# One core, 512 tokens, three layers in fp32 pairs: rotary angles earlier on VectorE, head norms of the second model part in another order, other counts of filler products at the layer norm

## The chip, the cores and the metric

The kernel runs on one core of one Trainium2 chip, as one program with one launch. The metric is the device time of that launch in microseconds, as the median of several runs. The five engines each work through an instruction stream of their own: TensorE (PE; its weight loads are listed as PEld), VectorE (DVE), ScalarE (ACT), GpSimd (POOL) and SyncE (SP), which here issues all transfers. They wait for each other through semaphores.

## The reference, cut to what matters

All of it is float32. x has 512 tokens of 1024 features.

```python
h = rms_norm(x, g[0])
proj = h @ w_in                      # gates, xs, q_lat (384), kv_lat (256), k_rope (32)
y_a  = gate_b * depthwise_conv(gate_c * xs, sc_kernel)
q    = rms_norm(q_lat, q_norm) @ w_uq
kv   = rms_norm(kv_lat, kv_norm) @ w_ukv
ang  = positions[..., None] * inv_freq
cos, sin = jnp.cos(ang), jnp.sin(ang)   # rotate q_pe and k_rope
x = x + rms_norm(concat(y_a, attention) @ w_out, g[1]);  x = x + rms_norm(mlp(...), g[3])
...
# second layer
u = a * sigmoid(g);  u = depthwise_conv(u, w_dw, 31 taps) + b_dw
u = silu(layer_norm(u, ln_g, ln_b));  m = u @ w_pw2 + b_pw2      # then rms_norm, mlp as above
...
# a third layer, behind 16 meta tokens
q, k, v, fg, u = split(rms_norm(h) @ w_in_2)
q, k = rms_norm over each head of 64;  cum_logf = cumsum(log_sigmoid(fg + b_fgate))
p_out = pool_scale * ((trailing_mean(u, 2/4/8/16) - u) @ w_pool)
h = h + concat(forgetting_attention(q, k, v, cum_logf), p_out) @ w_out;  h = h + swiglu(...)
```

## The kernel before

Everything is kept transposed: 128 features on the partitions, 512 tokens along the free axis. A weight block is 128 x 1024 floats (8 tiles of 128 x 128). For the precision each operand is held as a rounded high part and a low part, and a product of two tiles is three matmuls of 128 x 512 (`products`, L1646 to L1648): high x high, high x low, low x high. A weight block goes through a ring of four: SP loads `raw`, ScalarE rounds it to `wh` (`hi`), GpSimd subtracts to get `wl` (`lo`), TensorE uses both. A weight tile times all of x is 24 matmuls (`tile`). The results stand in four PSUM banks in turn; a tile can start when the one four tiles before it has been read out (`open_tile`, semaphore `bank_free`).

A norm is made of a few short steps that several engines share: the squares are summed to `ssq` (ScalarE and VectorE or GpSimd), TensorE sums over the partitions (`stat`, L1676), ScalarE takes the root (`root`, `latent_root`), VectorE the reciprocal (`factor`, L1081), and TensorE spreads the factors over the partitions (`spread`, L1688) with four matmuls (eight records, since these are fp32). `stat` and `spread` stand as hooks at hand-written places inside tiles. Where TensorE would have nothing to do, `keep_busy` issues products of an identity matrix into a spare bank (L1656); the counts are the constants `W_...` in one line (L126).

The order on each engine is written by hand; nothing is scheduled. Three places matter here.

The first is the start. VectorE makes the rotary angles (`angle`, L1054 to L1060 by its helpers): six or seven operations on 128 x 512, once for the cosine (`angle(0, 0.25)`, seven operations) and once for the sine (`angle(1, 0.0)`, six). Between the two it computes the reciprocal for x (`factor("x0")`) as soon as ScalarE has the root. Behind both stand the sums of squares of the latent q (`sum_squares`, L1052), which `stat("q_lat")` in tile 4 of w_in waits for. `spread("x0")`, earlier in tile 4, waits for that reciprocal. ScalarE's `latent_out` squares wait for x's sum.

The second is the layer norm in front of `pw2`. TensorE sums the mean (L1959), keeps busy (`W_CENTRE`), sums the squares over the features in four steps of four (L1976; GpSimd adds the pairs, L588), keeps busy for three (`W_FACTOR`), spreads, keeps busy for sixteen (`W_UPDATE`), and enters pw2. VectorE and ScalarE make the operand parts XH and XL of eight tiles meanwhile; `enter` runs three output tiles together over the input tiles as these arrive.

The third is w_in_2 of the third model part. Its tiles 0 to 3 are q of two heads each, tile 4 the forget gate (`log_forget`, `prefix_sums`), tiles 5 to 8 the pooled branch (`pool_tile`), 9 and 10 and two more in w_in_2b k of two heads each. Each of the eight head tiles needs a norm of its own: `head_square` and `head_root` (ScalarE), `head_stat` (TensorE, L2006), `head_factor` (VectorE, writes `hexp`, L1481 and L1482), `head_spread` (TensorE, L2017), `head_norm` (VectorE, L1060), `head_round` (ScalarE, L950), `head_low` (VectorE, L1060). TensorE's parts are hooks: head_stat(1) at k=2 and head_spread(1) at k=6 of tile 5, head_stat(2) and head_spread(2) at k=2 and k=7 of tile 6, head_stat(3) at k=4 of tile 7, head_spread(3) at k=2 of tile 8. head_stat(e) also waits for head_norm(e-1). Between tile 10 and w_in_2b stands the pool product: four groups of three matmuls into four banks, one `blocks_done` behind all; `pool_out` on VectorE scales the four results into `tmp` and `sqb` and frees the banks. The first tile of w_in_2b needs the first of these banks.

```python
            angle(0, 0.25)
            factor("x0")
            step(stt(floor[:], sd[:], EPS, sd[:], ALU.mult, ALU.mult))
            angle(1, 0.0)
```

Of the kernel before, what the change touches and what calls it, by code (L numbers as in the profile page):

```python
# [27 lines left out]
ALU = mybir.AluOpType  # L28
# [55 lines left out]
BLOCK0, TILE0 = {}, {}  # L84
# [38 lines left out]
HEAD_TILE = [TILE0["w_in_2"] + i for i in (0, 1, 2, 3, 9, 10)] + [TILE0["w_in_2b"] + i for i in range(2)]  # L123


W_STAT, W_FACTOR, W_UPDATE, W_MEAN, W_CENTRE, W_VALUES, W_START, W_GATE, W_WARM = 10, 3, 16, 10, 10, (1, 1), 20, 10, 8  # L126
P_OUT_STEPS = 4
Y_FREE = TILE0["w_in"] + 15

# [1 line left out]
def build(nc, x_t, meta_t, positions, vectors, weights, out_t):  # L131
    ctx = ExitStack()
    with ctx:
# [3 lines left out]
        def sem(name):  # L137
            return ctx.enter_context(nc.semaphore(name))
# [187 lines left out]
        p_out_h, p_out_l = sem("p_out_h"), sem("p_out_l")  # L326
        fz, fexp, cum_done, decay_q = sem("fz"), sem("fexp"), sem("cum_done"), sem("decay_q")
        pooled_done, pool_hi, pool_lo = sem("pooled_done"), sem("pool_hi"), sem("pool_lo")
        decay_ones, meta_zero = sem("decay_ones"), sem("meta_zero")
        decay_k = [sem(f"decay_k{e}") for e in range(HEADS // 2)]  # L330
        out_done = sem("out_done")
# [284 lines left out]
        def _(sc):  # L616
# [7 lines left out]
            def hi(n):  # L624
                if n >= NBLK:
                    return
                j = n % RING
                sc.wait_ge(raw_in[j], 16 * (n // RING + 1))
                if n >= RING:
                    sc.wait_ge(blocks_done, n - RING + 1)  # L630
                sc.activation(wh[:, j], raw[:, j], ACT.Copy).then_inc(w_hi, 1)  # L631
# [288 lines left out]
            def head_square(e):  # L920
                keys = e >= 4
                w = L2 if keys else S
                sc.wait_ge(bank_free, HEAD_TILE[e] + 1)
                if e:
                    sc.wait_ge(hstat, e)
                sc.activation(head_q[:, 0:w], head_t[:, e % 4, 0:w], ACT.Square).then_inc(hsq, 1)

            def head_root(e):

                keys = e >= 4  # L930
                scale = 1.0 if keys else float(HD)
                sc.wait_ge(hstat, e + 1)
                sc.activation(hcol[:, 0, 0:8], PS[:, STAT, 0:8], ACT.Sqrt, bias=EPS * scale,
                              scale=scale / HD).then_inc(act if keys else hsd, 1)
                if keys:
                    chain[0] += 1
                    sc.activation(hcol[0:META, 0, 8:10], PS[0:META, STAT, 8:10], ACT.Sqrt, bias=EPS * scale,
                                  scale=scale / HD).then_inc(hsd, 1)
# [15 lines left out]
            head_square(1)  # L954
            head_round(0)
            hi(n0 + 8)
            sc.wait_ge(fz, 1)
            sc.activation(logf[:, 1], logf[:, 1], ACT.Exp, scale=-1.0).then_inc(act, 1)
            chain[0] += 1
            sc.wait_ge(act, chain[0])  # L960
            sc.activation(logf[:, 1], logf[:, 1], ACT.Ln, bias=1.0).then_inc(fexp, 1)
            head_root(1)
            head_square(2)
            head_round(1)
            hi(n0 + 9)
            head_root(2)
# [70 lines left out]
        def _(v):  # L1037
# [8 lines left out]
            def sig(ins, s, n):  # L1046

                ins.then_inc(s, 1)
                v.wait_ge(s, n)
# [70 lines left out]
            def angle(i, shift):  # L1120

                step(ts(turns[:], ang[:], 0.15915494309189535, ALU.mult, shift, ALU.add))
                step(ts(turns[:], turns[:], 12582912.0, ALU.add, -12582912.0, ALU.add))
                for part in (6.28125, 0.0019350051879882812, 3.019916050461616e-07):
                    step(stt(trig[:, i], turns[:], -part, (ang if part > 6 else trig[:, i])[:], ALU.mult, ALU.add))
                if shift:
                    step(ts(trig[:, i], trig[:, i], 1.5707963267948966, ALU.add))
                sig(ts(trig[:, i], trig[:, i], 3.1415925, ALU.min, -3.1415925, ALU.max), angles, i + 1)
# [15 lines left out]
            step(v.tensor_copy(ang[:], pos_i[:]))  # L1144
            step(ts(ang[:], ang[:], col("inv_freq"), ALU.mult))
            angle(0, 0.25)
            factor("x0")
            step(stt(floor[:], sd[:], EPS, sd[:], ALU.mult, ALU.mult))
            angle(1, 0.0)

            T0, n0 = TILE0["w_in"], BLOCK0["w_in"]

# [395 lines left out]
                sig(stt(pooled[:, i], pool_a[:, i % 2, META:L2], 1.0 / w, u2[:, META:L2], ALU.mult, ALU.subtract),  # L1548
                    pooled_done, i + 1)

            def pool_out():

                for i in range(4):
                    T = TILE0["pool"] + i
                    v.wait_ge(blocks_done, BLOCK0["pool"] + 1)
                    sig(ts(p_out(i), PS[:, T % 4], col("pool_scale", i), ALU.mult), bank_free, T + 1)

            for e in range(4):
                head_in(e, "w_in_2", e)
# [5 lines left out]
            head_norm(1)  # L1565
            pool_tile(0)
            head_low(1)
            prefix_sums()
            head_factor(2)
            head_norm(2)  # L1570
            pool_tile(1)
            head_low(2)
# [6 lines left out]
            head_factor(4)  # L1579
            head_norm(4)  # L1580
            head_in(5, "w_in_2", 10)
            head_low(4)
            pool_out()
            head_factor(5)
            head_norm(5)
            head_in(6, "w_in_2b", 0)
# [56 lines left out]
        def _(pe):  # L1643
# [332 lines left out]
                    ins = pe.matmul(PS[:, STAT, j:j + 1], ln_sq[:, 2 * i, j * P:(j + 1) * P], ones[:, 0:1],  # L1976
                                    start=i == j == 0, stop=(i, j) == (LN_PAIRS - 1, 3))
            ins.then_inc(stat_done, 1)
            keep_busy(W_FACTOR, spare)
            spread("ln")  # L1980
            keep_busy(W_UPDATE, spare)
            enter("pw2", "ln")
            for m in range(4, KT):
                tile(BLOCK0["pw2"] + m, TILE0["pw2"] + m)
# [46 lines left out]
            for i in range(4):  # L2031
# [1 line left out]
                pe.wait_ge(pool_hi, i + 1)  # L2033
                pe.wait_ge(pool_lo, i + 1)
                ins = products(PS[:, (T1 + i) % 4], *weight(n1, i), pool_h[:, i], pool_l[:, i], True, True)
            ins.then_inc(blocks_done, 1)
            n0, T0 = BLOCK0["w_in_2b"], TILE0["w_in_2b"]
            for i in range(2):
                tile(n0 + i, T0 + i, {3: head(5 + i)[0], 6: head(5 + i)[1]}, meta_out=T0 + i)
# [203 lines left out]
```

## Time and profile before

| what | value |
|---|---|
| median of 3 runs | 1880.98 us (1879.87 to 1881.52) |
| the profiled execution | 1879.82 us |
| its span, first to last instruction | 1878.0 us |
| busy in the span: PE / DVE / ACT / POOL | 1820.3 / 809.6 / 636.8 / 900.8 us |
| granted TensorE clock, mean | 0.985 of full speed |

The page counts how long each engine worked, and follows the chain of waits back from the last instruction. A matmul of 128 x 512 is shown with 0.39 us, but such matmuls overlap, and in the chain each takes 0.23 us at full clock; at half clock 0.43 us. TensorE's granted clock stands per stretch: 1.00 is 2.4 GHz, 0.50 is 1.2 GHz. A wait in brackets at the end of a row, [1.64 <-DVE hexp L1482], says how long the engine was idle before and what ended that.

### The profile page before, as it was taken

Reading aid. Unit: us, or ns where it says so; the run is one execution under the profiler, and the core shown is the slowest. Engines: PE = TensorE matmul, PEld = TensorE weight load, DVE = VectorE, ACT = ScalarE, POOL = GpSimd, SP = SyncE. Lnnn points to the kernel's source line nnn. Section 1 sums busy time; section 2 is a strip of 40 time slices with the busy share of each in tenths; the row PEclk is TensorE's granted clock in tenths of the full one; section 3 lists DMA queues with packets and bytes.
Section 4 is the critical chain, followed back from the end, with each engine's and each line's share of the span. In section 5 each row is a group of like instructions: output and inputs, shape, how many; then the busy total and the mean of one; then the engine's idle time right before and its main releaser. Section 6 shows DMA issues by size and latency. Waiting matters only on the chain.

```text
span 1878.0 us, 23679 instructions
## 1 busy us (share of the span) xinstructions
PE 1820.3 (97%) x8511; PEld 1506.6 (80%) x8511; DVE 809.6 (43%) x1238; ACT 636.8 (34%) x954; POOL 900.8 (48%) x478
## 2 busy tenths in 40 slices
PE   7999999999999989999999999998998999999999
PEld 5787887888888768787888888887878778888887
DVE  7447645301321478855520232256546154444200
ACT  5327525222321444444321222252245242222221
POOL 5346445444444479954444444453243354444443
PEclk9999999999999989999999999998999999999999
DMA  5332022233232213221322322310210223322332
GB/s 176 85 121 68 12 90 79 90 101 96 93 101 92 66 56 102 68 88 61 109 95 95 101 91 99 100 57 24 81 57 1 68 68 101 101 94 96 101 103 76
DMA packets 45925, 157.87 MB, mean 84 GB/s; under 512 B 5728, under 2 KB 5984, under 8 KB 45856
## 3 DMA queue, kind: packets, MB, share of 16 engines
q1 hardware_dynamic: 45856, 156.93, 26.4%
q8 instruction: 46, 0.75, 0.2%
q14 instruction: 23, 0.19, 0.0%
HBM read 152.58 MB, written 2.10 MB: 82 GB/s over the span
## 4 chain that ended last, share of the span: by engine, by line
PE 86%; POOL 5%; DVE 5%; issue 2%; ACT 2%; DMA 0%; SPq 0%; POOLq 0%; DVEq 0%; ACTq 0%
PE PS L1646 27%; PE PS L1647 26%; PE PS L1648 26%; POOL acc_p L539 2%; PE PS L1656 2%; POOL wl L528 2%; PE PS L1857 1%; PE PS L1688 1%; PE PS L1676 1%; DVE PS L1060 1%; POOL acc_p L567 1%; PE PS L2017 1%; POOL UL L556 0%; DVE tmp L1060 0%; DVE XL L1052 0%
## 5 line engine op out<-in xcount | busy, mean ns | idle before, releaser
L475 POOL TENSOR_TENSOR wl<-raw,wh 128x1024 fp32r<-128x1024 f32 x232 | 563.0, 2428 | 677.0 <-ACT wh L645 293.1
L1646 PE MATMUL PS<-XH,wh 128*128 128x512 f32 x1408 | 561.2, 399 | 14.8 <-DVE PS L1056 5.0
L1647 PE MATMUL PS<-XL,wh 128*128 128x512 f32 x1408 | 552.3, 392 | 0.0
L1648 PE MATMUL PS<-XH,wl 128*128 128x512 f32 x1408 | 551.9, 392 | 0.0
L1646 PEld LDWEIGHTS PS<-XH,wh 128*128 128x128 f32 x1408 | 267.0, 190 | 78.5 <-issue 12.4
L1648 PEld LDWEIGHTS PS<-XH,wl 128*128 128x128 f32 x1408 | 266.7, 189 | 56.9
L1647 PEld LDWEIGHTS PS<-XL,wh 128*128 128x128 f32 x1408 | 267.0, 190 | 52.6
L1646 PE MATMUL PS<-HH,wh 128*128 128x512 f32 x688 | 267.6, 389 | 0.0
L1647 PE MATMUL PS<-HL,wh 128*128 128x512 f32 x688 | 267.6, 389 | 0.0
L1648 PE MATMUL PS<-HH,wl 128*128 128x512 f32 x688 | 267.6, 389 | 0.0
L645 ACT ACTIVATE wh<-raw 128x1024 fp32r<-128x1024 f32 x96 | 101.6, 1061 | 405.0 <-PE PS L1648 405.0
L1052 DVE TENSOR_TENSOR tmp<-PS,r 128x512 f32<-128x512 f32 x116 | 79.9, 691 | 236.2 <-PE PS L1648 215.9
L631 ACT ACTIVATE wh<-raw 128x1024 fp32r<-128x1024 f32 x94 | 98.6, 1055 | 154.6 <-PE PS L1648 146.0
L1648 PEld LDWEIGHTS PS<-HH,wl 128*128 128x128 f32 x688 | 129.1, 188 | 26.8
L1646 PEld LDWEIGHTS PS<-HH,wh 128*128 128x128 f32 x688 | 129.1, 188 | 26.8
L1647 PEld LDWEIGHTS PS<-HL,wh 128*128 128x128 f32 x688 | 129.1, 188 | 26.8
L466 POOL TENSOR_TENSOR wl<-raw,wh 128x1024 fp32r<-128x1024 f32 x33 | 80.5, 2446 | 131.1 <-ACT wh L631 131.0
L864 ACT ACTIVATE wh<-raw 128x1024 fp32r<-128x1024 f32 x56 | 59.4, 1060 | 164.2 <-PE PS L1648 164.2
L1031 ACT ACTIVATE wh<-raw 128x1024 fp32r<-128x1024 f32 x40 | 42.5, 1062 | 159.0 <-PE PS L1648 159.0
L496 POOL TENSOR_TENSOR prob<-prob,cols 128x512 f32<-128x512 f32 (+2 forms) x64 | 57.5, 901 | 64.4 <-DVE cols L1266 64.1
L1356 DVE COPY M<-PS 128x512 f32 x16 | 11.1, 692 | 158.6 <-PE PS L1648 158.6
L1052 DVE TENSOR_TENSOR X<-X,PS 128x512 f32<-128x512 f32 x16 | 11.0, 687 | 148.5 <-PE PS L1648 148.5
(310 smaller groups left out, 2302.0 us busy)
## 6 DMA issues: line engine op xcount, KB each, us to landing
raw<-weights SPq DMA_DIRECT2D x286, 512.0 KB, 3.5
X<-x_t SPq DMA_DIRECT2D x8, 256.0 KB, 6.8
out_t<-X SPq DMA_DIRECT2D x8, 256.0 KB, 4.4
KH<-rope_h SPq DMA_DIRECT2D x4, 128.0 KB, 4.6
KL<-rope_l SPq DMA_DIRECT2D x4, 128.0 KB, 5.3
QH<-XH SPq DMA_DIRECT2D x16, 32.0 KB, 2.0
QL<-XL SPq DMA_DIRECT2D x16, 32.0 KB, 2.0
pos_i<-positions SPq DMA_DIRECT2D x1, 256.0 KB, 9.3
```

Of the source, the lines that this page charges most:

```text
L466: pool.tensor_tensor(wl[:, n % RING], raw[:, n % RING], wh[:, n % RING].bitcast(F32), ALU.subtract).then_inc(w_lo, 1)
L475: pool.tensor_tensor(wl[:, j], raw[:, j], wh[:, j].bitcast(F32), ALU.subtract).then_inc(w_lo, 1)
L496: pool.tensor_tensor(p, p, cols[:, u % 4, 2:3].broadcast_to(p.shape), ALU.mult).then_inc(p_done, 1)
L528: pool.tensor_tensor(wl[:, i % RING], raw[:, i % RING], wh[:, i % RING].bitcast(F32), ALU.subtract).then_inc(w_lo, 1)
L631: sc.activation(wh[:, j], raw[:, j], ACT.Copy).then_inc(w_hi, 1)
L645: sc.activation(wh[:, j], raw[:, j], ACT.Copy).then_inc(w_hi, 1)
L864: sc.activation(wh[:, slot], raw[:, slot], ACT.Copy).then_inc(w_hi, 1)
L1031: sc.activation(wh[:, slot], raw[:, slot], ACT.Copy).then_inc(w_hi, 1)
L1052: return v.tensor_tensor(out, a, b, op)
L1646: pe.matmul(out, wa, xa, start=start, stop=False)
L1647: pe.matmul(out, wa, xb, start=False, stop=False)
L1648: return pe.matmul(out, wb, xa, start=False, stop=stop)
```

## The change

Five edits:

1. VectorE: `angle(1, 0.0)` is placed in front of `factor("x0")` and the `floor` operation, straight behind `angle(0, 0.25)`.
2. TensorE at the layer norm: `W_CENTRE` 16 for 10; the three products behind the squares' sum are dropped; the count behind the spread is `W_GATE` (10) for `W_UPDATE` (16).
3. ScalarE at w_in_2: head_root(1) and head_square(2) stand in front of the forget gate's Exp and Ln.
4. VectorE at w_in_2: head_factor(2) stands in front of `prefix_sums`, which now lies between head_factor(2) and head_norm(2).
5. The pool product counts each of its first three groups on a semaphore of its own (`pool_mixed`), and VectorE reads the results one by one, two of them in front of head_low(4), two behind it.

```diff
-W_STAT, W_FACTOR, W_UPDATE, W_MEAN, W_CENTRE, W_VALUES, W_START, W_GATE, W_WARM = 10, 3, 16, 10, 10, (1, 1), 20, 10, 8
+W_STAT, W_FACTOR, W_UPDATE, W_MEAN, W_CENTRE, W_VALUES, W_START, W_GATE, W_WARM = 10, 3, 16, 10, 16, (1, 1), 20, 10, 8
...
             head_round(0)
             hi(n0 + 8)
+            head_root(1)
+            head_square(2)
             sc.wait_ge(fz, 1)
             sc.activation(logf[:, 1], logf[:, 1], ACT.Exp, scale=-1.0).then_inc(act, 1)
...
             sc.activation(logf[:, 1], logf[:, 1], ACT.Ln, bias=1.0).then_inc(fexp, 1)
-            head_root(1)
-            head_square(2)
             head_round(1)
...
             angle(0, 0.25)
+            angle(1, 0.0)
             factor("x0")
             step(stt(floor[:], sd[:], EPS, sd[:], ALU.mult, ALU.mult))
-            angle(1, 0.0)
...
-            def pool_out():
-
-                for i in range(4):
-                    T = TILE0["pool"] + i
+            def pool_out(i):
+
+                T = TILE0["pool"] + i
+                if i == 3:
                     v.wait_ge(blocks_done, BLOCK0["pool"] + 1)
-                    sig(ts(p_out(i), PS[:, T % 4], col("pool_scale", i), ALU.mult), bank_free, T + 1)
+                else:
+                    v.wait_ge(pool_mixed, i + 1)
+                sig(ts(p_out(i), PS[:, T % 4], col("pool_scale", i), ALU.mult), bank_free, T + 1)
...
             head_low(1)
+            head_factor(2)
             prefix_sums()
-            head_factor(2)
             head_norm(2)
...
             head_in(5, "w_in_2", 10)
+            pool_out(0)
+            pool_out(1)
             head_low(4)
-            pool_out()
+            pool_out(2)
+            pool_out(3)
             head_factor(5)
...
             ins.then_inc(stat_done, 1)
-            keep_busy(W_FACTOR, spare)
             spread("ln")
-            keep_busy(W_UPDATE, spare)
+            keep_busy(W_GATE, spare)
             enter("pw2", "ln")
...
                 ins = products(PS[:, (T1 + i) % 4], *weight(n1, i), pool_h[:, i], pool_l[:, i], True, True)
-            ins.then_inc(blocks_done, 1)
+                ins.then_inc(blocks_done if i == 3 else pool_mixed, 1)
```

Where instructions move, the instruction streams show it. VectorE at the start, from the end of the first angle set to the sums of squares of the latent q; first before, then the change (its line numbers are one higher). `rcol` is x's factor, `turns` and `tmp` are the angles, `ssq` the sum.

```order
L1057 TENSOR_SCALAR tmp<-tmp 128x512
L1081 RECIPROCAL rcol<-sd 128x4
L1060 SCALAR_TENSOR_TENSOR floor<-sd 128x4
L1057 TENSOR_SCALAR turns<-ang 128x512
L1057 TENSOR_SCALAR turns<-turns 128x512
L1060 SCALAR_TENSOR_TENSOR tmp<-turns,ang 128x512
L1060 SCALAR_TENSOR_TENSOR tmp<-turns,tmp 128x512 x2
L1057 TENSOR_SCALAR tmp<-tmp 128x512
L1052 TENSOR_TENSOR PS<-PS,sqb 128x512
L1052 TENSOR_TENSOR ssq<-PS,sqb 128x512
```

```order
L1058 TENSOR_SCALAR tmp<-tmp 128x512
L1058 TENSOR_SCALAR turns<-ang 128x512
L1058 TENSOR_SCALAR turns<-turns 128x512
L1061 SCALAR_TENSOR_TENSOR tmp<-turns,ang 128x512
L1061 SCALAR_TENSOR_TENSOR tmp<-turns,tmp 128x512 x2
L1058 TENSOR_SCALAR tmp<-tmp 128x512
L1082 RECIPROCAL rcol<-sd 128x4
L1061 SCALAR_TENSOR_TENSOR floor<-sd 128x4
L1053 TENSOR_TENSOR PS<-PS,sqb 128x512
L1053 TENSOR_TENSOR ssq<-PS,sqb 128x512
```

The reciprocal and `floor` moved behind the six operations of the second set; nothing was added or taken away.

ScalarE at w_in_2, behind the first head's rounding; before, then the change. `hcol` is a head's root, `head_q` the squares of the next head, `logf` the forget gate's Exp and Ln, and ACT_TABLE_LOAD the load of another set of function tables.

```order
L631 ACTIVATE wh<-raw 128x1024
L958 ACT_TABLE_LOAD
L958 ACTIVATE logf<-logf 8x528
L961 ACT_TABLE_LOAD
L961 ACTIVATE logf<-logf 8x528
L933 ACT_TABLE_LOAD
L933 ACTIVATE hcol<-PS 128x8
L926 ACTIVATE head_q<-head_t 128x512
L950 ACTIVATE Q2H<-PS,headones 128x512 x2
L631 ACTIVATE wh<-raw 128x1024
L933 ACTIVATE hcol<-PS 128x8
```

```order
L632 ACTIVATE wh<-raw 128x1024
L934 ACTIVATE hcol<-PS 128x8
L927 ACTIVATE head_q<-head_t 128x512
L961 ACT_TABLE_LOAD
L961 ACTIVATE logf<-logf 8x528
L964 ACT_TABLE_LOAD
L964 ACTIVATE logf<-logf 8x528
L951 ACTIVATE Q2H<-PS,headones 128x512 x2
L632 ACTIVATE wh<-raw 128x1024
L934 ACT_TABLE_LOAD
L934 ACTIVATE hcol<-PS 128x8
```

The root of head tile 1 is now ahead of the three table loads; there are still three, the last of them in front of the root of head tile 2.

VectorE at w_in_2, between head_low(1) and head_norm(2); before, then the change. `hcol` and `hexp` are head_factor(2), the `logf` and `decay` rows are `prefix_sums`, the last row is head_norm(2).

```order
L1060 SCALAR_TENSOR_TENSOR logf<-logf 8x528
L1529 MEMSET logf 8x528
L1530 SCALAR_TENSOR_TENSOR logf<-logf 8x528
L1532 CAST decay<-logf 8x528
L1052 TENSOR_TENSOR decay<-logf,decay 8x528
L1481 RECIPROCAL hcol<-hcol 128x8
L1482 COPY hexp<-hcol 128x512
L1060 SCALAR_TENSOR_TENSOR PS<-head_t,vec,PS 128x512
```

```order
L1482 RECIPROCAL hcol<-hcol 128x8
L1483 COPY hexp<-hcol 128x512
L1061 SCALAR_TENSOR_TENSOR logf<-logf 8x528
L1530 MEMSET logf 8x528
L1531 SCALAR_TENSOR_TENSOR logf<-logf 8x528
L1533 CAST decay<-logf 8x528
L1053 TENSOR_TENSOR decay<-logf,decay 8x528
L1061 SCALAR_TENSOR_TENSOR PS<-head_t,vec,PS 128x512
```

The two operations of head_factor(2) went ahead of the five of the prefix sums.

## Rows read from the trace of the kernel before

**Rows 1.** Waits of PE, whole span: us in total, times, longest us.
```profile
PE PS L1676 <- DVE ssq L1052: 7.4, 1, 7.4
...
PE PS L2017 <- DVE hexp L1482: 4.8, 2, 3.2
...
PE PS L1646 <- DVE tmp L1056: 1.7, 1, 1.7
```

**Rows 2.** Timeline of DVE, 18 to 50 us: start us, us, line, operation, idle before.
```profile
27.57 0.69 DVE L1060 SCALAR_TENSOR_TENSOR tmp<-turns,ang 128x512 f32<-128x512 f32 x1
...
36.00 0.18 DVE L1081 RECIPROCAL rcol<-sd 128x4 f32<-128x4 f32 x1 [5.36 <-ACT sd L657]
...
42.14 5.46 DVE L1060 SCALAR_TENSOR_TENSOR tmp<-turns,tmp 128x512 f32<-128x512 f32 x2
...
48.83 0.69 DVE L1052 TENSOR_TENSOR ssq<-PS,sqb 128x512 f32<-128x512 f32 x1
```

**Rows 3.** Windows of PE at the start: us, busy (x), granted clock, DMA.
```profile
44.90:55.20 10.30, 5.62 (x17) 0.50 0.33 102
```

**Rows 4.** Timeline of POOL, 10 to 50 us.
```profile
32.74 2.40 POOL L466 TENSOR_TENSOR wl<-raw,wh 128x1024 fp32r<-128x1024 f32 x1 [13.99 <-ACT wh L631]
...
37.06 1.97 POOL L483 MEMSET KL<- 32x2048 f32 x1
```

**Rows 5.** Timeline of PE, 38 to 40 us: x's spread.
```profile
39.10 1.05 PE L1688 MATMUL PS<-ident,rcol 128*128 128x128 f32 x8
```

**Rows 6.** The chain in order of time, whole span: start us, us, what.
```profile
276.65 3.64 PE PS L1656 x16
...
807.06 1.49 PE PS L1656 x3
808.55 1.71 PE PS L1688 x8
810.26 4.96 PE PS L1656 x16
```

**Rows 7.** Timeline of DVE at the layer norm, 790 to 822 us.
```profile
807.30 0.18 DVE L1081 RECIPROCAL rcol<-sd 128x4 f32<-128x4 f32 x1 [3.86 <-ACT sd L657]
...
812.43 0.69 DVE L1052 TENSOR_TENSOR XL<-PS,XH 128x512 fp32r<-128x512 f32 x1 [0.73 <-ACT XH L912]
```

**Rows 8.** Windows of PE at the layer norm.
```profile
806.00:812.90 6.90, 6.90 (x24) 0.51 0.41 131
```

**Rows 9.** The chain, 1254 to 1296 us, third model part.
```profile
1264.43 1.28 ACT L958
...
1268.35 1.28 ACT L933
...
1270.64 2.08 PE PS L2017 x8
...
1281.94 0.99 DVE logf L1060
...
1286.80 1.58 PE PS L2017 x8
...
1295.27 0.79 PE PS L2006 x8
```

**Rows 10.** Windows of PE in the third model part.
```profile
1270.30:1273.70 3.40, 3.06 (x11) 0.50 0.00 0
...
1287.30:1294.20 6.90, 6.90 (x24) 0.51 0.00 0
```

**Rows 11.** Timeline of PE, 1254 to 1274 us: head_stat(1).
```profile
1263.96 0.95 PE L2006 MATMUL PS<-headones,head_q 128*128 128x2 f32 x8
```

**Rows 12.** Timeline of DVE, 1256 to 1345 us.
```profile
1329.80 0.69 DVE L1052 TENSOR_TENSOR head_t<-PS,r 128x512 f32<-128x512 f32 x1
...
1333.18 1.54 DVE L1056 TENSOR_SCALAR tmp<-PS,vec 128x512 f32<-128x512 f32 x2
```

**Rows 13.** Windows of PE behind the pool product.
```profile
1334.10:1340.00 5.90, 5.90 (x34) 1.00 0.62 180
```

More of the change, by code:

```diff
@@ L328, in build @@
         pooled_done, pool_hi, pool_lo = sem("pooled_done"), sem("pool_hi"), sem("pool_lo")
+        pool_mixed = sem("pool_mixed")
         decay_ones, meta_zero = sem("decay_ones"), sem("meta_zero")
```

## The prediction, made before the kernel ran

> **What bounds the kernel now.** I first read the page's shares: TensorE is busy for 1820.3 of the span's 1878.0 us, and the chain of waits runs through it almost everywhere. So a change can win in two ways only: a wait of TensorE that goes, or time in which its clock stands at half. I then listed the waits of TensorE by what ended them, and looked for those that the edits touch [rows 1]: 7.4 us for the latent q's sum of squares, 4.8 us in two waits for head factors (3.2 and 1.6), 1.7 us for the first scaled pool result. Last I read the granted clock around each. The reader is to see that a wait costs more than its length: behind it TensorE works at half clock for a while, and the same work at full clock takes half the time. VectorE is busy for 43% only; it matters by its order. A difference of 0.2% (3.8 us) is about what a measurement of this kernel can tell from none.
>
> **Part A, the angles.** VectorE has nothing to do for 5.36 us before x's factor, from 30.64 to 36.00 us, then makes the second angle set until 48.07, and the latent sums end at 49.52 [rows 2]. TensorE waits for them 7.4 us [rows 1], from 42.2 to 49.58. The clock is at 0.50 from 44.9 to 55.2 us [rows 3]; of that TensorE works 5.6 us, which would take 2.8 at full clock. So at most 7.4 + 2.8 = 10.2 us are to be had. To have all of it, the second set must be through before x's spread, which TensorE reaches at 38.9 [rows 5], with the sums before 42.2. The six operations cost 11.8 us where they stand now, but only since GpSimd works beside them: a scalar_tensor_tensor takes 0.69 us with GpSimd idle and 2.7 with GpSimd at work [rows 2]. GpSimd is idle until 32.74, then has a subtraction (2.40) and two memsets, the second 1.97 [rows 4]. From 30.66 the first four operations (two of about 0.45, two of 0.7) end near 33.0; the fifth waits for the subtraction and ends near 35.8; the sixth waits for the first memset and ends near 37.8. Factor and floor follow by 38.1, 0.8 us ahead of TensorE; the sums (1.45) have all they need from ScalarE by 39.8 and end near 41.3, 0.9 us ahead. **A = 10.2 us.** The bounds are 3.9 us, if the six take 11.8 us here too (they end at 42.5, the spread resumes at 42.7 and the latent statistic comes at 45.7), and 10.5, if the stretch at half clock has more in it than the windows show. I take the upper side since GpSimd's two idle microseconds at 30.7 are in the rows.
>
> The page GPSIMD Engine Reference of the Trainium skill, section Key points, says that GpSimd's SBUF interfaces are shared with VectorE, for VectorE instructions in a two-port mode or with two SBUF inputs. By it the angle operations collide, as the 2.7 us show, while the sums, which read PSUM, do not. If a memset, which reads nothing, did not collide either, the sixth operation would end 1.5 us earlier, and the sum would be the same.
>
> **Part B, the layer norm.** Six more products of `W_CENTRE` stand in time that waits for GpSimd's additions anyway: nothing. The squares' statistic ends at 807.06; then come three fillers (1.49), the spread (1.71), sixteen fillers (4.96, until 815.22) [rows 6]. The factor is there at 807.48 [rows 7], so without the three fillers the spread starts at 807.5 instead of 808.55: 1.05 us. It ends at 809.2. The clock is at 0.51 until 812.9 [rows 8]. Ten fillers at half clock (0.43 each, twice the 0.23 of 3.64 / 16 [rows 6]) end at 813.5; with the clock back at 812.9 as now, at 813.2. XL's first tile is ready at 813.12 now [rows 7], 1.05 earlier then, so pw2 can start. **B = 815.2 - 813.2 = 2.0 us.** The bounds are 1.7 (all at half clock) and 3.1 (TensorE waits for XL alone, at 812.1).
>
> **Part C, w_in_2.** *First spread.* ScalarE's chain of three table loads and the forget gate's two functions runs from 1264.43 to 1269.63, and the root that TensorE needs stands behind it [rows 9]. head_stat(1) is done at 1264.9 [rows 11]. With the root ahead, ScalarE gives it at 1265.1, VectorE finishes head_low(0) at 1266.4, and head_factor(1), its copy held up by GpSimd's subtraction, ends by 1267.5; TensorE comes at 1269.0 (1270.64 less 1.64). The wait of 1.6 us goes, and with it 3.06 us of work at half clock [rows 10], worth 1.5: 3.1 us. *Second spread.* VectorE's prefix sums and head_factor(2) fill 1281.94 to 1286.80 [rows 9], 4.9 us, of which the factor is 0.7. In a frame shifted by the 3.1 us, TensorE comes at 1280.5 and VectorE ends head_low(1) at 1278.8; the factor is there at 1279.6, 0.9 us early. The wait of 3.2 us goes and 6.90 us at half clock [rows 10], worth 3.4: 6.6 us. *What is late next:* head_norm(2) now stands behind the prefix sums, 1279.6 + 4.2 + 0.8 = 1284.6, and head_stat(3) waits for it. TensorE gets there 8.5 us behind the spread now (1286.80 to 1295.27 [rows 9]), 5.0 at full clock: 1285.5, again 0.9 us of slack. The third table load moves in front of head_root(2), which comes 0.2 us late by it, hidden by VectorE's later work. The forget gate's results come at 1269.6, ten us before VectorE asks. Prefix sums that end later delay only the decay rows, which are sent behind the fourth head tile and are needed by the attention. *Pool results.* The first tile of w_in_2b waits 1.7 us for the first scaled result [rows 1], which VectorE starts at 1333.18, behind head_low(4). Now it may start when head_in(5) ends at 1330.5 [rows 12], takes 0.77 and is out at 1331.3, before TensorE's 1332.4. head_low(4) is put off by 1.5 us, to 1334.7, and head_spread(5), which needs it, comes after 1339. The clock behind this wait is 1.00 [rows 13], so no more is won: 1.7 us. **C = 3.1 + 6.6 + 1.7 = 11.4 us.** The bounds are 1.7 (a new wait in the place of each) and 12.
>
> **Sum.** 10.2 + 2.0 + 11.4 = 23.6 us off the profiled execution's 1879.82 gives 1856.2; the median of the runs stands 1.2 us above that execution, so 1857.4 us.
>
> **The rivals.** *R1, VectorE becomes the bound in w_in_2.* Both slacks there are 0.9 us, and one more collision with GpSimd costs 2. For it: VectorE's row of pool and head operations is dense, and the prefix sums stand in front of everything that follows. Against it: ScalarE, GpSimd and TensorE all move up together. TensorE would then wait about 1.1 us, and the clock falls again, worth 3.4 as now: 4.5 us given back, 1861.9.
>
> *R2, GpSimd holds up the second angle set.* A falls to its lower bound of 3.9, with 6.3 given back: 1863.7. For it: the six took 11.8 us. Against it: only three GpSimd operations stand before 39 us, and VectorE starts two us ahead of the first.
>
> *R3, the edits do what they say but the clock falls at other places.* That is the slower case. A wait of 1.64 us at 1269 halved the clock [rows 10], an equal one at 1332 did not [rows 13]: which one does is a matter of where it falls. Moving 1850 us of program against the clock's switching could put falls in stretches that have none now (short waits in the attentions, at the layer boundaries). Each costs up to 3.4 us, as the stretch at 1287; from the seventh on the gain of 23.6 is gone, and eight give 1857.4 + 27.2 = 1884.6. For it: nothing that I can see in the rows. Against it: as many falls can go as come. The page TensorE: Matmul & The Clock Gate of the Trainium skill, section Part 1, says that the gate watches on a free-running beat that a kernel's start does not reset; by that rule the number of falls differs from run to run, and the 1.7 us between the three runs before leave little room for it.
>
> *R4, the clock does better.* By the same switching the fall at the layer norm, or one elsewhere, is shorter: B at its upper bound and one fall of 1.5 to 3.4 us less, 1853 to 1855.
>
> **How the numbers follow.** My forecast (1855 to 1860.5) has 0.67. R1 has 0.14, R2 0.08, R4 0.08, R3 0.02; 0.01 is left for no difference at all. The likeliest gives 1857. The range goes from 1853, R4's lower end, to 1864. Each case has an us or two of spread of its own, by the bounds of B and by where the clock switches, so of R4 and of R2, whose centres lie at the two ends, about half is inside; with the forecast and R1 that makes 0.85 or so. Faster by over 0.2% are all but R3 and the rest: 0.97. Within 0.2%: 0.01. Slower: 0.02.
>
> **What would show it.** Right: no wait of TensorE for `ssq` in the first 60 us and clock 1.00 there; `rcol` by 38.2 us; the layer norm's ten fillers end some 2 us earlier behind the statistic; no wait for `hexp`, clock 1.00 or nearly so through w_in_2; no wait for `tmp` at the first tile of w_in_2b. Wrong: TensorE waiting at x's spread (R2); a new wait at head_stat(3) or head_spread(3) for `head_n` or `hexp`, with a half-clock stretch behind it (R1); a lower mean clock than 0.985 with all these waits gone (R3). With no wait removed the mean clock would stay where it is; I expect 0.99 or more. The forecast is wrong as a whole if the waits go but the next engine's work, a weight's low part or a transfer, ends the same distance later; the rows show GpSimd and DMA with room at all three places.

## The result: 1863.6 us, and where the time went

The changed kernel took 1863.62 us (median of six runs, 1860.05 to 1870.37), the kernel before beside it 1881.25 us: a ratio of 0.9911, 95% interval 0.9894 to 0.9928. That is 17 us less, on the side that was forecast; the forecast was 1857, some 7 us too low. The time lies at the upper end of the range (1864): the ratio, laid on the 1880.98 us from which the forecast was made, gives 1864.2, just outside. The six runs are of two groups, four from 1860.05 to 1864.43 and two at 1870. The profiled execution took 1864.43 us, 8.2 more than the 1856.2 that the sum gave for it. Its span is 1862.6 us and its mean granted clock 0.990 (0.985 before).

The waits of TensorE over the whole span, for what [rows 1] showed (us in total, times, longest):

```profile
PE PS L1652 <- DVE sqb L1057: 2.6, 1, 2.6
...
PE PS L1652 <- DVE head_t L1053: 1.0, 1, 1.0
```

The waits for `ssq` at the start (7.4 us) and for `hexp` (4.8 in two) are gone, and so is the one for `tmp` (1.7). In its place stands a longer one, 2.6 us for `sqb`, the third pool result. The 1.0 us for `head_t` was there before too.

Next the chain of work that ended last (start us, us, what), at the points where it can be laid beside the chain before. Of the changed kernel:

```profile
33.73 1.59 PE PS L1752 x7
...
267.51 3.64 PE PS L1662 x16
...
796.43 1.23 PE PS L1982 x8
798.12 2.07 PE PS L1694 x8
800.20 4.11 PE PS L1662 x10
...
1243.89 0.79 PE PS L2011 x8
...
1274.56 0.79 PE PS L2011 x8
...
1300.40 0.98 PE PS L2011 x8
...
1330.58 0.98 PE PS L2011 x8
```

And of the kernel before, what the rows above leave out:

```profile
32.64 1.59 PE PS L1746 x7
...
805.60 1.46 PE PS L1976 x8
...
1254.79 0.79 PE PS L2006 x8
...
1321.10 0.98 PE PS L2006 x8
...
1347.27 0.98 PE PS L2006 x8
```

Subtract line from line. In this run the first work on x starts 1.09 us later than before, ahead of everything that was changed. The sixteen fillers of [rows 6] moved from 276.65 to 267.51: 9.14 us, so part A is 10.2 net of that. From the squares' statistic to pw2 it was 9.62 us (805.60 to 815.22) and is 7.88 (796.43 to 804.31): part B is 1.74. Over w_in_2's head tiles the distance to before grows from 10.90 (1254.79 less 1243.89) to 20.71 us (1295.27 [rows 9] less 1274.56): 9.8 for the two `hexp` waits. It is still 20.70 at head_stat(4), 1321.10 less 1300.40. At head_stat(6) it is 16.69 (1347.27 less 1330.58), and at the end of the span 15.4. So everything came until 1300 us, and 4.0 + 1.3 us were given back behind it.

TensorE where they were given back (start, us, line, operation, idle before), in the first tile of w_in_2b:

```profile
1315.97 0.39 PE L1654 MATMUL PS<-XH,wl 128*128 128x512 f32 x1
1318.93 0.28 PE L1652 MATMUL PS<-meta_h,wh 128*128 128x16 f32 x1 [2.57 <-DVE sqb L1057]
...
1320.41 0.63 PE L1653 MATMUL PS<-XL,wh 128*128 128x512 f32 x1
```

VectorE in front of that wait, and GpSimd beside it:

```profile
1309.82 1.54 DVE L1057 TENSOR_SCALAR tmp<-PS,vec 128x512 f32<-128x512 f32 x2
1311.39 0.23 DVE L1057 TENSOR_SCALAR K2H<-head_t,headones 128x16 fp32r<-128x16 f32 x1
1311.67 2.26 DVE L1061 SCALAR_TENSOR_TENSOR K2L<-head_t,headones,K2H 128x16 fp32r<-128x16 f32 x1
1313.96 2.29 DVE L1057 TENSOR_SCALAR K2H<-head_t,headones 128x16 fp32r<-128x16 f32 x1
1316.28 0.23 DVE L1061 SCALAR_TENSOR_TENSOR K2L<-head_t,headones,K2H 128x16 fp32r<-128x16 f32 x1
1316.56 1.54 DVE L1061 SCALAR_TENSOR_TENSOR K2L<-PS,headones,K2H 128x512 fp32r<-128x512 f32 x2
1318.13 1.54 DVE L1057 TENSOR_SCALAR sqb<-PS,vec 128x512 f32<-128x512 f32 x2
```

```profile
1311.49 4.73 POOL L467 TENSOR_TENSOR wl<-raw,wh 128x1024 fp32r<-128x1024 f32 x2 [8.30 <-ACT wh L632]
```

Two things are to be seen. First, the matmul that waits is narrow, 16 columns of `meta_h`: the tile computes the meta tokens' columns too, from its fifth step on. In front of the first of them stands a wait, unchanged by the edits:

```python
                        if k == KT // 2:
                            pe.wait_ge(bank_free, meta_out - 1)
```

`bank_free` counts the read-outs in the order of the tiles, and this asks for all of them up to the tile two before. For w_in_2b's first tile that is the pool product's third result, and its read-out now stands behind head_low(4). The matmuls don't need that bank: the meta columns go to banks 5 and 7 in turn (`meta_bank`), the pool results stand in banks 0 to 3. It is the count that makes TensorE wait; a kernel that asks for a smaller count was not run.

Second, head_low(4) itself got longer. Its first four operations are only 128 x 16; two of them take 2.3 us, beside GpSimd's two subtractions, which start at 1311.49. Before, the same four stood ahead of GpSimd's start (1332.20), and VectorE's timeline had them at 0.23 and 0.24 us each:

```profile
1330.53 0.23 DVE L1056 TENSOR_SCALAR K2H<-head_t,headones 128x16 fp32r<-128x16 f32 x1
1330.80 0.24 DVE L1060 SCALAR_TENSOR_TENSOR K2L<-head_t,headones,K2H 128x16 fp32r<-128x16 f32 x1
...
1334.75 1.54 DVE L1056 TENSOR_SCALAR sqb<-PS,vec 128x512 f32<-128x512 f32 x2
```

```profile
1332.20 4.71 POOL L466 TENSOR_TENSOR wl<-raw,wh 128x1024 fp32r<-128x1024 f32 x2 [8.30 <-ACT wh L631]
```

The row at 1334.75 is the third and fourth pool result, the one below it GpSimd's two subtractions.

The page GPSIMD Engine Reference of the Trainium skill, section Key points, names the forms that collide with GpSimd: two SBUF inputs, or a two-port mode. The trace agrees for K2L, which has two SBUF inputs (`head_t` and `K2H`), and for operations that read PSUM: in the kernel before, `tmp` and `sqb` (1333.18 and 1334.75) take 0.77 us each beside the two subtractions, and in the version with the small operations first, below, the two large `K2L` take 1.54 together (from 1314.12). The blocked K2H has one SBUF input, `head_t`; that it ran in a two-port mode, no row says.

The clock behind the wait (windows of TensorE: us, busy (x), granted clock, DMA):

```profile
1319.70:1326.10 6.40, 6.40 (x24) 0.50 0.45 168
1340.00:1342.70 2.70, 2.68 (x6) 0.50 0.00 0
```

6.4 us at half clock cost 3.2. With the wait 0.9 us longer than the one it replaces, that is the 4.0 us. A second fall, 2.7 us long, stands behind the 1.0 us wait for `head_t` and costs the last 1.3. It does not come from the fifth edit: the kernel without it, below, has it too.

### The profile page after: what moved, and what is told of

The parts are those of the page before. It is cut to its first block, busy times and chain, and to the rows that moved or that the text cites. A ratio compares the mean times of both kernels' runs of the same rounds, so it can differ in the third digit from the quotient of the medians.

```text
span 1862.6 us, 23673 instructions
## 1 busy us (share of the span) xinstructions
PE 1817.0 (98%) x8508; PEld 1503.9 (81%) x8508; DVE 806.4 (43%) x1238; ACT 636.6 (34%) x954; POOL 899.8 (48%) x478
## 4 chain that ended last, share of the span: by engine, by line
PE 87%; POOL 5%; DVE 4%; issue 2%; ACT 1%; DMA 0%; SPq 0%; POOLq 0%; DVEq 0%; ACTq 0%
PE PS L1652 27%; PE PS L1654 27%; PE PS L1653 27%; POOL acc_p L540 2%; PE PS L1662 2%; POOL wl L529 2%; PE PS L1863 1%; PE PS L1694 1%; POOL acc_p L568 1%; DVE PS L1061 1%; PE PS L1682 1%; POOL UL L557 1%; PE PS L2022 0%; PE PS L1745 0%; DVE XL L1053 0%
```

## The experiments

Each part alone first. The four kernels ran on one chip and have the same runs of the kernel before beside them (median 1880.51 us).

**The angles alone** (edit 1).

```diff
             angle(0, 0.25)
+            angle(1, 0.0)
             factor("x0")
             step(stt(floor[:], sd[:], EPS, sd[:], ALU.mult, ALU.mult))
-            angle(1, 0.0)
```

> The kernel before with the first edit alone (second angle set ahead of x's factor). Theory 1 (the sum of part A: 7.4 us of waiting and 2.8 us of half clock): 10.2 us less, about 1871; no wait of TensorE for ssq in the first 60 us, clock 1.00 there, x's spread on time. Rival (GpSimd holds up the six operations): 4 us less, about 1877, with a wait at x's spread.

1870.75 us (1869.58 to 1877.61), ratio 0.9952, interval 0.9938 to 0.9966: 9.0 us. Three of its nine runs were at 1875 to 1878. The profiled one was among these, and its window from the first `hexp` wait (which this kernel still has) shows why:

```profile
1261.90:1291.80 29.90, 29.90 (x100) 0.50 0.05 18
```

Behind a wait of 1.64 us TensorE stayed at half clock for 29.9 us, where [rows 10] had 3.4. In most runs it did not.

**The layer norm alone** (edit 2).

```diff
-... W_CENTRE = 10
+... W_CENTRE = 16
-            keep_busy(W_FACTOR, spare)
             spread("ln")
-            keep_busy(W_UPDATE, spare)
+            keep_busy(W_GATE, spare)
```

> The kernel before with the second edit alone (filler counts at the layer norm). Theory 1: the spread starts 1.05 us earlier and ten fillers at about half clock end 1.7 to 2.0 us earlier behind the squares' statistic; 1879.2 us. Rival (the clock is worse without the fillers): half clock reaches into pw2's products, and the time is that of before or 1 us above. From the one first profile of the change the gain is 1.7.

1876.89 us, ratio 0.9980, interval 0.9961 to 0.9998: 3.8 us with 0.4 to 7 possible. The chain gives the size that the times can't. From 806.73 to pw2 at 814.61 it is 7.88 us, as in the whole change:

```profile
806.73 1.20 PE PS L1976 x8
808.39 2.08 PE PS L1688 x8
810.47 4.14 PE PS L1656 x10
```

**The head norms alone** (edits 3 and 4).

```diff
             hi(n0 + 8)
+            head_root(1)
+            head_square(2)
             sc.wait_ge(fz, 1)
...
-            head_root(1)
-            head_square(2)
             head_round(1)
...
+            head_factor(2)
             prefix_sums()
-            head_factor(2)
```

> The kernel before with edits 3 and 4 alone (root of head tile 1 ahead of the forget gate, factor of head tile 2 ahead of the prefix sums). Theory 1: both waits for hexp (4.8 us) go and with them 10 us at half clock, 9.7 us less, about 1871. Rival: one new wait at head_stat(3) or head_spread(3) with a fall of the clock, 5 us less.

1869.73 us (1868.48 to 1870.58), ratio 0.9936, interval 0.9914 to 0.9959: 12.0 us, against 9.8 by the trace of the whole change, which is inside the interval. No wait for `hexp` is left.

**The pool results alone** (edit 5).

```diff
             head_in(5, "w_in_2", 10)
+            pool_out(0)
+            pool_out(1)
             head_low(4)
-            pool_out()
+            pool_out(2)
+            pool_out(3)
```

> The kernel before with the fifth edit alone (pool results read one by one, two ahead of head_low(4)). Theory 1 (the meta columns of w_in_2b's first tile wait for the third pool result, which stands behind head_low(4), and that is held up by GpSimd's two subtractions): the wait of 1.7 us at the tile's start goes, one of about 2.5 us comes in its middle, and the clock falls behind it: 0.9 + 3.2 = about 4 us slower, 1885. Rival (the wait seen in the changed kernel was an effect of everything else having moved): 1.7 us less, 1879.3, no wait in the tile's middle.

1883.80 us (1881.84 to 1891.25), ratio 1.0018, interval 1.0006 to 1.0031: this part alone makes the kernel slower, by 3.4 us, where 1.7 were to be won. Its waits name the same new one, and its VectorE shows the same collision. The granted clock is below 1.00 for 3 to 4 us behind that wait (0.77, 0.50, 0.50 and 0.53 in the four us from 1342), not for 6.4.

```profile
PE PS L1652 <- DVE sqb L1057: 2.6, 1, 2.6
```

```profile
1332.90 2.26 DVE L1061 SCALAR_TENSOR_TENSOR K2L<-head_t,headones,K2H 128x16 fp32r<-128x16 f32 x1
1335.20 2.29 DVE L1057 TENSOR_SCALAR K2H<-head_t,headones 128x16 fp32r<-128x16 f32 x1
```

Then the fifth edit was taken apart, in four kernels with one set of runs of before beside them (median 1879.04 us).

**The change without edit 5.** The diff is the one above, undone.

> The changed kernel without its fifth edit: pool results as before, all four behind head_low(4), one signal. Theory 1 (the three other parts add up, and the fifth edit costs): 10.2 + 1.7 + 9.7 = 21.6 us below the kernel before, 1859, some 4 us below the changed kernel; the wait of 1.7 us for the first pool result is there, none in the tile's middle. Rival (the parts share time, so that together they give less than alone): 1863 as the changed kernel.

1860.54 us (1859.23 to 1861.25), ratio 0.9890, interval 0.9869 to 0.9911. The wait for `tmp`, 1.7 us, is back, and its runs lie within about 2 us. Behind the wait for `tmp` the clock stays at 1.00; behind the 1.0 us for `head_t` it falls (0.86 and 0.85 over 1332 to 1338 and 1338 to 1344), as in the change. Against the version with the small operations first (1857.56 us, below) that is 3.0 us, about the 1.7 of the wait and the 1.3 of this fall.

**Three results ahead of head_low(4).**

```diff
             pool_out(0)
             pool_out(1)
-            head_low(4)
             pool_out(2)
+            head_low(4)
             pool_out(3)
```

> The changed kernel with the third pool result read ahead of head_low(4) too (order 0, 1, 2, head_low(4), 3). Theory 1 (the loss is VectorE's: four small operations of head_low(4) cost 5 us instead of 1 since they fall together with GpSimd's two subtractions): the wait in the middle of w_in_2b's first tile goes, and one of 1.5 to 2.5 us comes at its head_spread(5), for hexp; the time stays within 1.5 us of the changed kernel's, 1862 to 1864. Rival (the loss is the order alone: the third result stands behind head_low(4)): no wait in this tile, 2.6 + 3.2 = 5.8 us less, 1858.

1860.59 us, but from 1858.43 to 1874.16; ratio 0.9912, interval 0.9881 to 0.9944. The third result is in time. The small operations collide as before (1.74 and 2.30 us), and it is the fifth spread that TensorE waits for:

```profile
PE PS L2020 <- DVE meta_x L1488: 2.0, 1, 2.0
```

So the order alone moves the wait; the collision makes it. Behind this wait of 2.0 us the clock stayed at 1.00 in the profiled run (1320 to 1326), yet two of the six runs took 1870.72 and 1874.16 us: the upper group of times is not the 2.6 us wait's alone. These two have no profile.

**The four small operations first.**

```diff
+            head_low(4, rest=False)      # the four 128x16 operations
             pool_out(0)
             pool_out(1)
-            head_low(4)
             pool_out(2)
+            head_low(4, meta=False)      # the two 128x512 operations
             pool_out(3)
```

> The changed kernel with head_low(4) in two parts: its four small operations straight behind head_in(5), while GpSimd is idle, then pool results 0, 1, 2, then the two large ones, which read PSUM, then pool result 3. Theory 1 (collision): the small ones take 0.25 us each, TensorE waits at most 0.3 us at the tile's start and no more in it, the clock stays at 1.00: 6 to 7 us less than the changed kernel, about 1857. Rival (VectorE is too full here in any order): a wait of 1 us or more at head_spread(5) with a fall of the clock, 1860 to 1863.

1857.56 us (1855.99 to 1858.29), ratio 0.9874, interval 0.9853 to 0.9895: better than the change and than the kernel before. VectorE:

```profile
1310.68 0.23 DVE L1057 TENSOR_SCALAR K2H<-head_t,headones 128x16 fp32r<-128x16 f32 x1
...
1311.49 0.23 DVE L1061 SCALAR_TENSOR_TENSOR K2L<-head_t,headones,K2H 128x16 fp32r<-128x16 f32 x1
1311.76 1.54 DVE L1057 TENSOR_SCALAR tmp<-PS,vec 128x512 f32<-128x512 f32 x2
1313.33 0.75 DVE L1057 TENSOR_SCALAR sqb<-PS,vec 128x512 f32<-128x512 f32 x1
```

GpSimd starts at 1312.35 here, when all four are done, and the results, read from PSUM, keep their time. This version changes two things, the place of the small operations and that of the third result ahead of the large ones. By its rows the first alone would have done: with the two large ones (1.54 us) in front of it, the third result would be out near 1315.7, and TensorE's first narrow matmul stands at 1317.40 (an estimate from rows; it was not run). No wait for a pool result is left, and the clock is full through w_in_2b, the 1.0 us for `head_t` included:

```profile
1316.00:1338.00 22.00, 21.01 (x130) 1.00 0.22 74
```

**The change again**, beside the three.

> The changed kernel once more, beside the three others on one chip. Theory 1 (its scatter comes from where the clock falls): median 1860 to 1866, the waits of TensorE as in its first profile to 0.1 us, and what differs is the mean clock. Rival (there are waits that come and go): another list of waits.

1869.87 us (1869.04 to 1871.12), ratio 0.9942, interval 0.9923 to 0.9961. The waits are those of the first profile, and two small ones at the start: 0.29 us for `rcol` at x's spread and 0.24 for `ssq`. The stretch at half clock behind the 2.6 us is not:

```profile
1317.80:1337.80 20.00, 20.00 (x70) 0.50 0.24 81
```

20 us in place of 6.4: 6.8 us more, of the 5 to 10 us between this median and the 1860 to 1864.4 of the lower runs. The rest of the span has its half clock at the same places in both profiles, but for one stretch of 3.4 us at 10 us, ahead of the first work on x. The same program with the same wait thus gave two groups of times, 1860 to 1864.4 and 1869 to 1871. The next kernel asks whether that wait makes both.

**The wait filled.** Products of the identity matrix run in its place, in front of the tile's fifth step.

```diff
-                tile(n0 + i, T0 + i, {3: head(5 + i)[0], 6: head(5 + i)[1]}, meta_out=T0 + i)
+                hooks = {3: head(5 + i)[0], 6: head(5 + i)[1]}
+                if i == 0:
+                    hooks[4] = lambda: keep_busy(11, PS[:, meta_bank(T0 + 1)])
+                tile(n0 + i, T0 + i, hooks, meta_out=T0 + i)
```

> The change as it is, with eleven filler products into the spare bank in the middle of w_in_2b's first tile, where TensorE otherwise waits 2.6 us for the third pool result. The wait itself stays covered (the products end about when the result is out), so nothing is won by length. Theory 1 (the run-to-run scatter of the change, 1860 to 1870, is half clock behind that wait): granted clock near 1.00 behind it, ratio 0.988 to 0.990 (1858 to 1861), no run at 1870. Theory 2 (the scatter comes from elsewhere, the wait costs its own 2.6 us and no more): runs at 1870 still occur, the median stays at the change's 1862 to 1870.

1859.03 us (1858.27 to 1860.03), ratio 0.9887, interval 0.9866 to 0.9907; no run near 1870. TensorE across the place:

```profile
1314.27 2.67 PE L1662 MATMUL PS<-ident_r 128*128 128x512 f32 x11
...
1317.69 0.28 PE L1652 MATMUL PS<-meta_h,wh 128*128 128x16 f32 x1
```

and its windows:

```profile
1314.00:1320.00 6.00, 5.92 (x33) 1.00 0.05 15
1320.00:1326.00 6.00, 6.00 (x37) 1.00 0.47 165
...
1338.00:1344.00 6.00, 6.00 (x33) 1.00 0.30 90
```

The third result is as late as it was, and nothing useful is done in these 2.6 us; but the clock stays at 1.00, behind the wait for `head_t` as well. So the wait's length costs 2.6 us, against the version without it (1856.39 us, measured beside this one, below). What it cost beyond that is half clock: by the profiles 3.2 us for the 6.4 at half clock and 10 for the 20. The change itself was not run beside this kernel; the interval lies clear of the change's second measurement (0.9923 to 0.9961) and overlaps its first (0.9894 to 0.9928). That the wait makes the upper group is what five runs without one of it, and the clock at 1.00, bear out.

**Ten products for the layer norm's centre, one filler between the squares' groups, and the best version again.** These three were measured beside the kernel with the wait filled (kernel before 1878.81 us), all from the version with the small operations first.

```diff
-... W_CENTRE = 16
+... W_CENTRE = 10
```

> The version with the small head operations first (1857.56 us, ratio 0.9874 to the kernel before), with W_CENTRE back from 16 to 10 products. Theory 1 (the six more products stand in time that waits for GpSimd's additions and hold nothing that matters): same time within 0.5 us of that version. Theory 2 (they keep the clock up for the squares' sums): the clock falls earlier at the layer norm, +1 to +2 us.

```diff
+                if i < LN_PAIRS - 1:
+                    keep_busy(1, spare)
```

> The version with the small head operations first, with one filler product between each two of the four groups of the squares' statistic at the layer norm. Theory 1 (the half clock there, from the statistic to pw2, is what is left to win, and a denser TensorE keeps it away): spread and fillers at full clock, up to 3 us less than that version (1854.5). Theory 2 (the half clock has its cause in the statistic's own thin matmuls or before it): no gain, 0 to +0.5 us.

> The version with the small head operations first once more, beside the others of this call. Expected: ratio to the kernel before 0.987 to 0.989, all its runs within 3 us, no wait of TensorE for a pool result or a head value in w_in_2b.

The times were 1856.99, 1856.99 and 1856.39 us, the ratios 0.9872, 0.9874 and 0.9873 (intervals 0.985 to 0.990). The six extra products do nothing that shows, as the prediction had it. The filler between the groups doesn't hold the clock either; the windows of that kernel at the layer norm:

```profile
792.00:796.00 4.00, 4.00 (x31) 1.00 0.15 59
796.00:800.00 4.00, 3.52 (x18) 0.58 0.19 16
800.00:804.00 4.00, 4.00 (x13) 0.57 0.74 245
```

It still falls near 797 us, though TensorE was busy for all of 792 to 796. What would keep it up there stays open: no kernel was made with other work in place of the thin matmuls of statistic and spread. The best version holds in both its measurements: five runs each, 1855.6 to 1858.3 us.

## Why the prediction was wrong, and where it was right

The step that failed is the last term of part C, the pool results: forecast as 1.7 us won, measured as 4.0 lost in the profiled run. The other terms (A, B and the two spreads of C) came out within 0.3 us. The second measurement of the same program gave 1869.87 us: that the first median lies at the range's end, and not well above it, is luck, since four of its six runs were of the lower group. That it stands near R1's 1861.9 and R2's 1863.7 is chance too; neither happened as written.

**Part A was right: 10.2 us forecast, 10.2 measured** net of the later start. The row of VectorE:

```profile
33.18 3.60 DVE L1061 SCALAR_TENSOR_TENSOR tmp<-turns,tmp 128x512 f32<-128x512 f32 x2
36.81 1.56 DVE L1058 TENSOR_SCALAR tmp<-tmp 128x512 f32<-128x512 f32 x1
38.40 0.18 DVE L1082 RECIPROCAL rcol<-sd 128x4 f32<-128x4 f32 x1
```

The fifth operation waited for the subtraction and the sixth for the first memset, as laid out; the reciprocal is there at 38.58, TensorE at 40.19, 1.6 us of slack where 0.8 was expected. That slack is this run's. In the second measurement's profile GpSimd's subtraction started at 31.76 us, held up the third operation (2.76 us) and not the fifth, and the last one stood beside the second memset; the reciprocal came at 38.51, TensorE at 38.28, and it waited 0.29 us. The clock there, at 0.50 before, is 1.00 (the window below). R2, in which GpSimd holds the set up, did not come here, and in the second profile with 0.5 us of waiting only (0.29 and 0.24).

**Part B: 2.0 forecast, 1.74 measured**, at the lower bound of 1.7. The ten fillers ran at about half clock (4.11 us, where half clock throughout is 4.3): the clock came back near 804 us, 7.6 behind the statistic's start, before it was 7.3 ([rows 8]). R4, a shorter fall, did not come. (The prediction's "0.43 each, twice the 0.23" is a slip of words: 0.43 us is what a product takes in the rows at half clock, and the sum uses it rightly.)

**Part C's two spreads were right: 9.7 forecast, 9.8 measured.** Both `hexp` waits went, and the half clock with them. The windows of TensorE at the start and over the head tiles:

```profile
44.00:55.00 11.00, 11.00 (x57) 1.00 0.60 188
1250.00:1300.00 50.00, 50.00 (x311) 1.00 0.13 44
```

TensorE is busy throughout in both. The two slacks of 0.9 us on VectorE held, and so did the new order behind them: head_stat(3) follows without a wait. R1 as it was placed, in w_in_2, did not come.

**Part C's pool results failed: 1.7 forecast, -4.0 measured.** Two steps of it are wrong. The first is "The first tile of w_in_2b waits 1.7 us for the first scaled result", read as the only thing for which that part of TensorE's order waits. I followed the one wait that the trace showed, and not the next: in front of the same tile's narrow matmuls TensorE waits until `bank_free` has counted the third result, which the change puts behind head_low(4). Before, that result was started at 1334.75, 1.6 us behind the first (the first at 1333.18 in [rows 12]), and was out while the tile worked on its first steps. The second is "head_low(4) is put off by 1.5 us". Its four small operations moved out of GpSimd's idle time into its two subtractions, and went from 0.9 us together to 5.1 (1311.39 to 1316.51). The collision was priced at 2 us in R1, for w_in_2, and left out here. So the mechanism of R1 happened, at a place where I had not looked for it. The 5.7 us between +1.7 and -4.0 are the 2.6 us of the wait and the 3.2 of the half clock, to a tenth.

**"The clock behind this wait is 1.00 [rows 13], so no more is won"** was true of the 1.7 us wait. It was no warrant for another one in the middle of the tile. And the 1.0 us wait for `head_t`, behind which the clock stayed at 1.00 before, now cost 1.3 us. The prediction put that at nothing. Why the clock fell there is open: it fell in the kernel without edit 5 too, where no fall stands ahead of it, and not in the version with the small operations first.

**R3 said too little of the clock.** Its price for a fall (up to 3.4 us) was taken from one profiled execution. The runs show 6.4, 20 and 29.9 us at half clock behind waits of 2.57 and 1.64 us. The page TensorE: Matmul & The Clock Gate of the Trainium skill, section Part 1, has the gate watch on a free-running beat that a kernel's start does not reset, and the prediction set this aside on the 1.7 us between three runs. The runs agree in so far as one program gave different stretches, 6.4 and 20 us behind the same 2.6 us wait. They don't show the beat itself, nor why one stretch is three times the other.

In the profiled execution the gap of 8.2 us closes as 1.1 (later start), 0.3 (B), -0.1 (C's spreads), 5.7 (pool results) and 1.3 (second fall), 8.3 together. With the fifth edit put right, in the version with the small operations first, the kernel takes the 1857 us that the sum gave (1857.56 and 1856.39 in two measurements).

## What to carry to other kernels

When results are handed over one by one in a new order, list for every one of them which waits count it and when, not only for the one that the trace shows a wait on; the next late one may hide behind the present wait. A count can ask for more than the data need, as here. Small SBUF operations of VectorE belong where GpSimd is idle: 0.9 us of them cost 5.1 beside two subtractions, and the version with them ahead took 1857.56 us, against 1863.62 and 1869.87 for the change in its two measurements. And price a wait of TensorE by its length plus a stretch at half clock that one profile does not bound: where a wait can't be avoided, fillers in it are worth trying; here they kept the clock at 1.00.

## What the runs showed of the hardware

- The stretch at half clock behind one and the same wait is not a constant: 6.4 and 20.0 us behind 2.6 us in two executions of the same program, 29.9 us (all of it busy) behind 1.64 us, where the kernel before had 3.4. In all three TensorE went on with tiles in which matmuls of 16 columns stand between those of 512. So it did in the kernel before, and behind the 2.0 us wait of the version with three results ahead, where the clock stayed at 1.00. Whether these matmuls have a part in it was not tried.
- The same short wait halves the clock in one kernel and not in another. Behind the 1.0 us for `head_t` it stayed full in the kernel before, with the wait filled and with the small operations first; it fell in the change, in the change without edit 5, and in the version with three results ahead (0.90 and 0.82 over 1332 to 1338 and 1338 to 1344).
- A memset of GpSimd, which reads nothing, held up a TENSOR_SCALAR of VectorE on SBUF: the last angle operation took 1.56 us, 0.43 alone, and ended 0.3 us after the memset (36.28 to 38.08 us). The prediction had left that open. It did not hold up operations with two SBUF inputs: in the profile of the second measurement two SCALAR_TENSOR_TENSORs of 128 x 512 took 1.42 us together (from 34.88) beside a memset from 34.35 to 36.15, as they do alone, while the TENSOR_SCALAR behind them took 1.97 beside the next memset.
- The size of a blocked operation hardly mattered: 128 x 16 took 2.26 and 2.29 us beside the subtractions, nearly one subtraction each (2.36), in place of 0.23; in the profile of the second measurement 128 x 512 took 2.76 for 0.69 beside one of 2.53.
